# The first pair of experts takes its rows from x on chip through a one-hot product, and its swish goes ahead of the list tables

## The reference

```python
def hier_moe(h, ...):                      # h = RMSNorm(x), 576 rows
    g_idx = argmax(h @ wg_r + bg_r)        # 1 of 4 groups
    elog_g = (h @ we_r + be_r)[group g_idx]
    top_v, top_i = top_k(elog_g, 2)        # 2 of the 8 experts of the group
    gate = softmax(top_v) * softmax(group logits)[g_idx]
    # 32 experts; an expert runs on the rows that chose it
    y = sum over the chosen experts of gate * ((silu(h @ w_gate[e]) * (h @ w_up[e])) @ w_down[e])
x = x + y
```

## Time and profile before

| | us |
|---|---|
| median of 3 runs | 1164.77 (1164.1 to 1165.12) |
| the profiled execution, its own time | 1165.38 |
| its span, first to last instruction | 1163.6 |
| PE busy | 1032.4 (89%) |
| DVE busy | 458.5 (39%) |
| ACT busy | 186.1 (16%) |
| POOL busy | 113.1 (10%) |

### The profile page before, as it was taken

How to read it: one execution, slowest core, us unless ns; L and a number is a source line. 1 busy time by engine, 2 the same in 40 slices (tenths; PEclk the granted TensorE clock), 3 DMA queues, 4 the chain that set the end, 5 groups by cost and what they waited for, 6 DMA issues and landing times.

```text
span 1163.6 us, 11497 instructions
## 1 busy us (share of the span) xinstructions
PE 1032.4 (89%) x4528; PEld 540.7 (46%) x4528; DVE 458.5 (39%) x770; ACT 186.1 (16%) x486; POOL 113.1 (10%) x167
## 2 busy tenths in 40 slices
PE   6999999999999999999998699987876889887880
PEld 3577744555445446777656343333332233333320
DVE  4169645563664024013227743322222233322224
ACT  0156233433113101012101000000000000000001
POOL 1200001132016000000000010010000000100002
PEclk9999999999999999999998699999989899989995
DMA  8221130312233433212085599999999999999977
GB/s 254 73 73 54 45 123 1 134 52 82 74 108 103 177 145 145 73 57 89 1 355 200 220 397 427 427 427 426 428 427 426 422 427 427 426 427 427 413 297 251
DMA packets 56548, 277.50 MB, mean 238 GB/s; under 512 B 13360, under 2 KB 15280, under 8 KB 44336
## 3 DMA queue, kind: packets, MB, share of 16 engines
q1 hardware_dynamic: 43648, 256.01, 54.7%
q10 hardware_dynamic: 7808, 11.32, 2.7%
q0 software_dynamic: 5040, 9.45, 2.2%
HBM read 273.34 MB, written 18.61 MB: 251 GB/s over the span
## 4 chain that ended last, share of the span: by engine, by line
PE 69%; DMA 18%; DVE 6%; SPq 4%; issue 2%; ACT 0%; POOL 0%; ACTq 0%; DVEq 0%; POOLq 0%
PE bank L497 23%; DMA arena<-in_exp_w_down_dram 15%; PE bank L485 13%; PE bank L882 12%; PE bank L872 6%; SPq L1089 4%; PE bank L501 2%; PE bank L747 2%; PE score_pair L721 2%; PE bank L635 1%; DVE arena L1675 1%; DMA arena<-expert_rows 1%; PE score_pair L551 1%; PE bank L585 1%; DMA arena<-in_w_in_dram 1%
## 5 line engine op out<-in xcount | busy, mean ns | idle before, releaser
L497 PE MATMUL bank<-arena 128*128 128x512 f32 x640 | 285.0, 599 | 2.6 <-DMA arena<-in_w_in_dram 1.9
L882 PE MATMUL bank<-arena 128*64 128x512 f32 x1024 | 238.3, 622 | 38.5 <-issue 35.2
L497 PEld LDWEIGHTS bank<-arena 128*128 128x128 f32 x640 | 119.7, 191 | 147.0 <-issue 145.5
L882 PEld LDWEIGHTS bank<-arena 128*64 128x64 f32 x1024 | 83.4, 143 | 190.6 <-issue 189.4
L485 PE MATMUL bank<-arena 128*128 128x288 f32 x640 | 156.1, 406 | 0.0
L872 PE MATMUL bank<-arena 128*64 128x512 f32 x512 | 119.5, 621 | 26.6 <-DMA arena<-in_exp_w_down_dram 19.5
L485 PEld LDWEIGHTS bank<-arena 128*128 128x128 f32 x640 | 121.4, 190 | 33.8 <-issue 0.4
L1298 ACT ACTIVATE arena<-bank 128x512 f32<-128x512 f32 (+6 forms) x135 | 61.7, 493 | 378.3 <-PE bank L497 112.5
L872 PEld LDWEIGHTS bank<-arena 128*64 128x64 f32 x512 | 39.9, 142 | 95.1 <-issue 83.5
L1521 ACT ACTIVATE arena<-bank,arena 128x512 f32<-128x512 f32 x17 | 11.7, 687 | 428.3 <-PE bank L882 404.4
L2045 DVE SCALAR_TENSOR_TENSOR arena<-bank,arena 128x512 f32<-128x512 f32 x34 | 25.5, 751 | 109.8 <-PE bank L872 102.8
(11 more groups left out here) (295 smaller groups left out, 928.1 us busy)
## 6 DMA issues: line engine op xcount, KB each, us to landing
arena<-in_exp_w_gate_dram SPq DMA_DIRECT2D x30, 2048.0 KB, 33.0
arena<-in_exp_w_up_dram SPq DMA_DIRECT2D x30, 2048.0 KB, 37.7
arena<-in_exp_w_down_dram SPq DMA_DIRECT2D x28, 2048.0 KB, 34.7
arena<-in_w_in_dram SPq DMA_DIRECT2D x7, 2048.0 KB, 8.5
out_dram<-arena SPq DMA_DIRECT2D x4, 1024.0 KB, 10.5
arena<-in_w_mem_k_dram SPq DMA_DIRECT2D x2, 2048.0 KB, 10.3
arena<-in_w_mem_v_dram SPq DMA_DIRECT2D x2, 2048.0 KB, 8.6
arena<-in_w_out_dram SPq DMA_DIRECT2D x2, 2048.0 KB, 12.7
```

The source lines that it names most:

```text
L497: ins = mm(b[:, :], x, w[:, k, :], start=k == 0, stop=k == KC - 1)
L882: ins = mm(bank[own, :], xgT[:, k, own], w[j][:, k, :], start=k == 0, stop=k == KC - 1)
```

## The change

- **Rows of pair 0.** They are no longer gathered for its products. DVE's `near_rows` compares the ranks, read from PSUM, with 64 slot numbers for each of the experts 0 to 3 and so makes one-hots of token and slot. The ranks' matrix gets -1024 on its diagonal for this, so that only a row that chose the expert can match. PE's `place_x` multiplies x, tile by tile, by the one-hots of experts 0 and 1: the result is the turned rows of pair 0, in one bank of each PSUM ring. Tiles 0 to 2 go ahead of the last choice, tiles 3 and 4 behind it.
- **Ranks** are taken in three portions instead of two, and `sel_ready` is raised for each.
- `near_tokens` now multiplies by two values (token number and 1/std) for each of two pairs, in `score_pair`.
- **DVE's order.** `copy_rows` of pair 0 stands ahead of `near_row`; the swish of pair 0 and `copy_rows` of pair 1 stand ahead of the places and lists; `read_lists` and `passes_needed` stand ahead of the drain of pair 0.
- **PE's order.** `all_lists` goes from pair 0 to pair 1, between its up product and the turn of pair 2's rows.
- **SP.** The last two loads of pair 1's gate and up parts change places: the one that overwrites tile 0 of x waits for `place_x` of tile 0 (`x0_read`).
- **ACT** no longer waits for the lists' one-hots before the exponential of pair 0.
- The gather of pair 0's rows stays, for the addition at its drain. Some scratch areas move.

```diff
@@ -206,14 +208,12 @@
 
         xg = [area(40960 + 1024 * i, 1024) for i in range(3)]
         xg_rows = [x.rearrange("p (d k) -> p k d", k=KC) for x in xg]
-        xgT = area(44032, KC, P)
+        hET = area(44032, 4, P)
+        xgT = [area(OZ + 4672, 4, P), area(44544, 4, P)]
         eG = area(OZ, 512)
-        hET = area(OZ + 512, 4, P)
-        hE = area(OZ + 1024, 512)
-        hE_rows = hE.rearrange("p (d k) -> p k d", k=4)
-        gS2 = area(OZ + 1536, 512)
+        hE_rows = eG.rearrange("p (d k) -> p k d", k=4)
+        xo = area(OZ + 1024, 1024)
         yS = [area(OZ + 2048 + 1024 * i, 1024) for i in range(2)]
-        xo = area(OZ + 4096, 1024)
         xo_rows = xo.rearrange("p (d k) -> p k d", k=KC)
 
         yg = [[area(1024 * (2 * t + k), 1024) for k in range(2)] for t in range(NT)]
...
@@ -806,11 +806,19 @@
 
             def near_tokens(a, b):
 
-                for k in range(2):
-                    for t in range(a, b):
-                        rows = TILES[t][1]
-                        ins = mm(near_list, hot_s[0:rows, k, t, :], list4[0:rows, k, t].rearrange("p v i -> p (v i)"), start=k == 0 and t == 0,
-                                 stop=k == 1 and t == SAMPLE, skip_group_check=True)
+                for t in range(a, b):
+                    rows = TILES[t][1]
+                    for i in range(2):
+                        ins = mm(near_list[:, 2 * i:2 * i + 2], near_hots[0:rows, t, i, :], near_vals[0:rows, t, :], start=t == 0 and i == 0,
+                                 stop=t == SAMPLE, skip_group_check=True)
+                return ins
+
+            def place_x(t, ks):
+
+                rows = TILES[t][1]
+                for k in ks:
+                    ins = mm(first_rows[k // 4][:, (k % 4) * P:(k % 4 + 1) * P], x_cols[t][0:rows, k, :], near_hots[0:rows, t, 0, :],
+                             start=t == 0 and k % 4 == 0, stop=t == SAMPLE, skip_group_check=True)
                 return ins
 
             LOW, HIGH = range(4), range(4, KC)
...
@@ -837,19 +845,32 @@
             router(4, LOW)
             proj_N(16, actT, SAMPLE, V)
             router(3, HIGH)
+            pe.wait_ge(sel_ready, 2)
+            first_rows = [A.banks[(A.filled - 1) % 3], V.banks[(V.filled - 1) % 3]]
+            mark["first_rows"] = first_rows
+            ranks(2, 3)
+            pe.wait_ge(a_free, A.filled)
+            pe.wait_ge(near_hot, 1)
+            place_x(0, LOW)
             turn_x(4, 1)
+            place_x(0, HIGH).then_inc(x0_read, 1)
             router(4, HIGH)
-            pe.wait_ge(near_hot, 1)
-            near_list = A.open(pe)[:, 0:4]
-            mark["near"] = A.filled % 3
-            near_tokens(0, 2)
-            pe.wait_ge(sel_ready, 2)
-            ranks(2, NT)
+            place_x(1, range(KC))
             pe.wait_ge(near_hot, 2)
-            near_tokens(2, NT).then_inc(near_full, 1)
+            place_x(2, range(KC))
+            pe.wait_ge(lg_read, NT)
+            near_list = pair[:, 0, 256:260]
+            near_tokens(0, 3)
+            pe.wait_ge(sel_ready, 3)
+            ranks(3, NT)
+            pe.wait_ge(near_hot, 3)
+            for ks in (LOW, HIGH):
+                place_x(3, ks)
+                place_x(4, ks).then_inc(SP_.tx_full, 1)
+            pe.wait_ge(near_hot, 4)
+            near_tokens(3, NT).then_inc(near_full, 1)
 
             pe.wait_ge(v_free, V.filled)
-            pe.wait_ge(a_free, A.filled)
 
             def turn_rows(S, rows):
...
@@ -919,8 +940,6 @@
 
             for signal in (SO.g_full, SO.u_full, SO.dn_full):
                 pe.sem_inc(signal, 1)
-            pe.wait_ge(xg_ld[0], 16)
-            turn_rows(SP_, xg_rows[0])
             for i in range(PAIRS):
                 w = pass_weights(i)
...
@@ -939,11 +958,13 @@
                     landed(2)
                     landed(3)
                     from_rows(SP_, i, banks[1], w[2:4], SP_.u_full)
+                if i == 0:
+                    pe.wait_ge(near_std, 1)
+                if i == 1:
+                    all_lists()
                 if i + 1 < PAIRS and i != OVER_AFTER:
                     pe.wait_ge(xg_ld[(i + 1) % 3], 16 * ((i + 1) // 3 + 1))
                     turn_rows(SP_, xg_rows[(i + 1) % 3])
-                if i == 0:
-                    all_lists()
                 turn_h(SP_, i)
                 pe.wait_ge(SP_.hT_cp, i + 1)
                 if i < PAIRS - 1:
...
@@ -1064,10 +1085,11 @@
             s, n = unit_done[16]
             sp.wait_ge(s, n)
             load_part(1, 0, 2)
-            sp.wait_ge(x_st0, 16)
-            load_part(1, 3, 3)
             sp.wait_ge(lg_full, NT)
             load_part(1, 2, 2)
+            sp.wait_ge(x_st0, 16)
+            sp.wait_ge(x0_read, 1)
+            load_part(1, 3, 3)
 
             def freed(i, m, over):
...
@@ -1154,7 +1176,9 @@
             n.step(g.memset(bdmask, 1))
             n.step(g.iota(dist_i, pattern=[[-1, 512]], base=SEQ - P, channel_multiplier=1))
             n.settle()
-            n.step(g.affine_select(out=upper, in_=upper, pattern=[[1, P]], compare_op=ALU.is_gt, fill=0.0, base=0, channel_multiplier=-1))
+            n.link(g.affine_select(out=upper, in_=upper, pattern=[[1, P]], compare_op=ALU.is_gt, fill=0.0, base=0, channel_multiplier=-1))
+            n.step(g.affine_select(out=upper, in_=upper, pattern=[[1, P]], compare_op=ALU.not_equal, fill=-PICKED, base=0,
+                                   channel_multiplier=-1))
             n.step(g.affine_select(out=bdmask, in_=bdmask, pattern=[[1, P]], compare_op=ALU.is_ge, fill=0, base=0, channel_multiplier=-1))
             n.settle()
             bd3 = bdmask.rearrange("p (j c) -> p j c", j=4)
...
@@ -1525,11 +1549,11 @@
                 f(rows, rows, ACT.Copy, scale=own).then_inc(signal, 1)
 
             act.wait_ge(near_std, 1)
-            act.wait_ge(hot_ready, 2)
             for i in range(PAIRS):
                 exp_gate_rows(SP_, i, 0, near[:, 0, 0:1] if i == 0 else table[:, 0, i:i + 1])
                 if i == 0:
                     act.wait_ge(table_ready, 1)
+                    act.wait_ge(xg_ld[0], 16)
                 own_rows(xg[i % 3], table[:, 2, i:i + 1], xm_ready)
                 if i == OVER_AFTER:
                     def over_pair(n):
...
@@ -1908,28 +1932,22 @@
                         n.link(last)
                 return last
 
-            def near_slots(a, b):
+            def near_rows(a, b):
 
                 c, nt = slice(a, b), b - a
                 bank = V.take(ve)
                 got = bank[:, 0:nt * NE].rearrange("p (t e) -> p t e", e=NE)
-                n.step(ts(own4[:, c], got[:, :, 0:4], float(CAP), None, ALU.is_lt))
-                n.step(tt(rank4[:, c], got[:, :, 0:4], per_tile(half4, nt), ALU.add))
-                if b < NT:
-                    V.done(v.tensor_copy(rank[:, c], got))
-                n.settle()
-                n.link(tt(valid4[:, :, c], oh[:, :, c, 0:4], twice(rank4[:, c]), ALU.mult))
-                n.link(red(lo_f[:, :, c], valid4[:, :, c], AX_X, ALU.add))
-                n.step(tt(hot_s[:, :, c], iota_s.unsqueeze(1).unsqueeze(1).broadcast_to([P, 2, nt, P]), wide(lo_f[:, :, c], P), ALU.is_equal))
-                return bank
-
-            def near_values(a, b):
-
-                c = slice(a, b)
-                n.link(tt(valid4[:, :, c], oh[:, :, c, 0:4], twice(own4[:, c]), ALU.mult))
-                n.link(red(pair4[:, :, c], valid4[:, :, c].rearrange("p k t (i j) -> p k t i j", j=2), AX_X, ALU.add))
-                n.step(tt(list4[:, :, c, 0], pair4[:, :, c], twice(wide(tokv[:, c], 2)), ALU.mult))
-                tt(list4[:, :, c, 1], pair4[:, :, c], twice(wide(rstd[:, 12 + a:12 + b], 2)), ALU.mult).then_inc(near_hot, 1)
+                for es in ((0, 4),) if b < NT else ((0, 2), (2, 4)):
+                    if es[1] == 4:
+                        n.step(v.tensor_copy(near_vals[:, c, 1], rstd[:, 12 + a:12 + b]))
+                    shape = [P, nt, es[1] - es[0], CAP]
+                    tt(near_hots4[:, c, es[0]:es[1], :], wide(got[:, :, es[0]:es[1]], CAP),
+                       near_iota.unsqueeze(1).unsqueeze(1).broadcast_to(shape), ALU.is_equal).then_inc(near_hot, 1)
+                ins = ts(rank[:, c], got, PICKED, None, ALU.add)
+                if b == NT:
+                    n.step(ins)
+                    ins = v.tensor_copy(cnt, bank[:, nt * NE:(nt + 1) * NE])
+                V.done(ins)
 
             add_stats(0)
             add_stats(1)
...
@@ -1939,20 +1957,29 @@
             choose(0, 2).then_inc(sel_ready, 1)
             add_stats(3)
             router_logits(2)
-            n.link(choose(2, 3))
-            near_slots(0, 2)
+            near_rows(0, 2)
+            choose(2, 3).then_inc(sel_ready, 1)
             add_stats(4)
-            near_values(0, 2)
+            near_rows(2, 3)
             router_logits(3)
             router_logits(4)
             choose(3, NT).then_inc(sel_ready, 1)
```

(73 more changed lines are left out.)

48 lines of the change are left out of this document (25 added, 23 removed).

## The result

The changed kernel takes 1176.62 us at the median of 4 runs (1172.42 to 1177.62), the kernel before 1164.64 beside it: a ratio of 1.0098, interval 1.008 to 1.0115. It is slower by 12 us where 7 us faster was forecast, and outside the range. The profiled execution took 1177.62 us, its span is 1175.8.

A forecast was written before the change was run, and what follows sets the result against it. The prediction took the DMA stream of weights to bound the kernel: idle DMA time falls from 12.9 to 6.0 us, a gain of 6.9, so the median becomes 1157.9, said as 1158.0 us; range 1154.3 to 1165.5.

The forecast's parts named there:

- Ahead of the last choice: Step on PE's work before the choice: a place_x tile costs 1.9 us, logits taken at 634.9, choice ends at 640.5.
- the three signs: Wrong if strided passes cost over 0.145 at full clock, the gather over 8 us, or DVE's order is late for pair 2.
- Tiles 1 and 2 (3.8 us) fit on PE below this: Before the ranks: place_x of these tiles was to fit on PE while DVE made the last choice.
- T: Start of pair 0's first gate product, 655.14 before; forecast 649.5, at best 646.4 and at worst 652.2.
- the first gap: Idle DMA time around 647 to 666 us, while SP's issue waits for pair 0's gate product; forecast 6.0 us lost.
- at T = 646.4 and the full clock: Case that PE keeps the full clock: idle 2.8, gain 10.1, time 1154.7; chance 0.17.
- the half clock through `place_x`: Case that the half clock lasts through place_x and gate: T = 652.2, gain 3.4, time 1161.4; chance 0.12.
- The case that I held likeliest: The forecast itself, clock lost and regained during place_x: 1158.0, own range 1156 to 1160.5; chance 0.45.
- The other side: Case that PE waits at pair 1 for pair 2's gathered rows: 1165 at the median gather, 1169 at the longest; chance 0.18.
- The bound: The stream of weights sets the end; an edit ahead counts only by DMA time given back or lost, at most 12.9 us.
- The gap at 684: Idle DMA at 684 to 688 us, 0.5 us; claimed to close as all_lists leaves pair 0.
- The swish ahead of the tables: Pair 0: claimed to cost nothing, with the order ready at T + 9.1 and the swish done at T + 13.8.

The follow-up runs named there:

- e12: e8 with the packing taken out, so x's columns are strided, early lists and eight busy products kept; 1169.4 us.
- e1: The changed kernel with x cut into packed columns for place_x, pair 0's gate and up weights and gain laid out to match; 1167.97 us.
- e3: The changed kernel with packed columns and with the lists' products between pair 1's gate and up products; 1161.9 us, ratio 0.9975 to the kernel before.
- e8: e3 plus eight unread products that fill TensorE's two waits, for the last choice and the last one-hots; 1155.86 us, ratio 0.9924 to the kernel before.
- e4: The changed kernel with tables, lists and swish in the order of the kernel before; pair 0's rows still placed, strided columns; 1172.3 us.
- e7: e4 with packed columns; 1164.9 us, ratio 1.0007 to the kernel before.
- e10: The changed kernel with pair 0's rows gathered instead of placed, early lists, and 60 unread products before the wait for the first gather; 1168.5 us.
- e2: The changed kernel with the lists' products moved from behind pair 1's up product to between its gate and up products; 1169.2 us.

## Why the prediction was wrong

**The failed step** is under "Ahead of the last choice": "Contiguous passes take 3.73 / 32 = 0.117 us; the turn, whose stationary operand is strided as here, 1.16 / 8 = 0.145 us." I bounded a pass of `place_x` by 0.117 and 0.145. It took 0.247 in a group of 32, and, from one start to the next inside a group, 0.238 us at the granted clock 1.00 and 0.240 at 0.50. The clock hardly matters to it. In the kernel after, the 32 passes of tiles 1 and 2 ran from 637.99 to 645.89, and these windows show the clock at 0.50 in the first half and at 1.00 at the end:

```profile
636.00:642.00 6.00, 6.00 (x30) 5.71 (x29) 3.29 (x17) 0.00 (x0) 0.00 (x0) 0.50 0.87 320
...
644.00:645.80 1.80, 1.80 (x10) 1.80 (x10) 0.00 (x0) 0.00 (x0) 0.00 (x0) 1.00 1.00 428
```

They took 7.90 us; the same passes took 7.88 in e12 at 1.00 throughout. A packed pass follows the last after 0.112 us at 1.00 and 0.213 at 0.50 (e1). The load of a block with a step of eight elements takes 335 ns against 192, and at either clock the loads of strided blocks leave no gap (8.00 of 8.00 us in e12): I read from this that they set the pace. The Trainium skill has a rule that I should have weighed: SBUF — State Buffer, section Door 1: The DMA port swizzle, says that on-chip memory is read in lines of 16 bytes and that only a step of up to four float32 values is free. Here the step was 32 bytes, and e1 and e12 agree with it: packing halves the pass at full clock. Whether these lines are the reason, no run shows; the runs show the step's price. Two of the three signs that the prediction names as proof against it came true, this one and the gather over 8 us; the third, a late order, did not.

**What followed on PE.** Ahead of the ranks stand 48 passes. The last logits, forecast at 634.9, were taken at 638.10; "Tiles 1 and 2 (3.8 us) fit on PE below this" failed too, for they took 7.9 and held the ranks back 3.4 us behind a choice that was ready. The 40 passes behind the ranks took 10.8 us, where my bound at the half clock was 10.0. T was 658.85, beyond my worst of 652.2. Idle DMA time in the first gap was 13.7 us where I had 6.0.

**With packed columns the step holds.** e1's T is 650.98 (forecast 649.5, own bounds 646.4 and 652.2), e3's 646.40. And the times of my cases come out, once the lists are early as well: at T = 646.4 and the full clock I wrote 1154.7, e8 gives 1155.9; with the half clock through `place_x` I wrote 1161.4, ten of e3's executions lie at 1160.7 to 1163.9. The case that I held likeliest, lost and regained within `place_x`, was not seen in a packed kernel. In the kernel after the clock did come back at about 642.3, within the strided passes, and fell again at about 649.1.

**The other side, the late gather**, came on top, 7.1 us of idle DMA time, where I had given it 0.18. With the first gap's 7.7 us beyond the forecast that is 14.8 of the 18.6 us between 1158.0 and 1176.6. I took 7.3 us to landing and the rule of the Trainium skill (DMA: Bandwidth & Descriptors, Queues, rings and completion order) as a reason not to take more. It landed after 10.9 us. The same lone gather landed after 10.6 to 10.9 us in the kernel after and ten of the twelve others, all with the DMA engines full, and after 5.4 (e4) and 4.9 (e7) in the two where their share fell below 0.4 within 6 us of it; the 7.3 of the earlier trace rows stood shortly ahead of the dip at 684. So I had read its price off the one execution whose DMA engines were about to run short of work; that this made it short fits e4 and e7, but was not tested by itself. How much of the 10.9 is queueing, and where, no run tells; the rule may be true and its consequence for a gather of many rows still be this. My working of that case gave T + 53.0 + 10.9 = T + 63.9 for the next loads; they flowed at T + 67.3, since the gather was issued 1.7 us later than I had it and the down product ran 1.7 us longer, partly at the half clock. The DMA engines ran dry at about T + 61, as forecast. The chances of this case were also at odds with its own prices: the median gather of 15.3 us gives 1165, which can't be told from the kernel before, and only one of more than 17 us would have been slower, yet 0.12 of the 0.18 stood under slower. By the shares of the cases, same is 0.14 and slower 0.12, where the text has 0.13 for each.

**What held.** The bound: an edit counts by the DMA time that it gives back or loses (the table's span less idle). The price of a later T: 6.3 us for 7.1 (e10), 8.7 back for 6.8 (e1). The gap at 684 closed. The swish ahead of the tables cost nothing: the order was ready at 667.67, T + 8.8, and the down product of pair 0 started at T + 18.4, 1.8 us later than forecast, as the gate product began at the half clock. The initial loads ended some 2 us later than forecast (the last two were issued at 638.09), which softened the first gap. A gain of the forecast's size (6.9 us; e8 is 8.4 us faster than the kernel before, run beside it) came only with three things that the change did not have: packed columns, early lists, and a TensorE that does not idle twice.

## What to carry to other kernels

Before a pass is priced by a neighbour, look at its load as well as at its length, and at how far apart the elements lie that it loads; a one-hot product has a large stationary operand, and packing it may need only another order of rows in the first weights. Work that is meant to fill an engine's wait stands in that engine's queue: if it is twice as long as thought, it holds back the small step on which everybody waits. And when a gather is made ready just in time, price it by examples that met full DMA engines, not by the one that met a dip.

## What was unexpected of the hardware

- A float32 block with a step of eight elements loads into TensorE in 335 ns, a packed one in 192. Strided passes follow each other every 0.238 us at the granted clock 1.00 and every 0.240 at 0.50; packed ones every 0.112 and 0.213. So the step costs a factor of 2.1 at the full clock and 1.1 at the half one, and to the strided passes the clock gave nothing.
- Passes that alternate between 128 and 64 rows cost more: the 32 of tiles 3 and 4, in four groups of 8, took 4.32 us packed and 8.89 strided (e8; e2, at 0.50), where the 32 of tiles 1 and 2 took 3.84 and 7.88. The excess, 0.2 to 0.3 us, lies at each change of tile.
- The clock fell from 2.4 to 1.2 GHz while PE stood busy without a gap: in e12 PE is busy for all of 647.3 to 655.8 us with strided passes, and the granted clock is 1.00 to 650 us and 0.76 in the mean of the rest, so it fell at about 653. In the kernel after it fell at about 635.5, among strided passes; in e2, whose work is the same up to there, it stayed at 1.00 until about 646.3.
- Whether two waits of 0.5 to 0.6 us cost the clock differed between executions of one and the same kernel (e3: 2 of 12 kept it, by their times and mean clocks), and that was worth 6 us; with the waits filled all five executions kept the shorter time.
- A lone gather of 0.5 MB took 10.6 to 10.9 us to land in eleven kernels where the DMA engines stayed full, 7.3 in the kernel before, and 5.4 and 4.9 where their share fell below 0.4 on its way.
